# The token router before the expert stage: handovers between TensorE, VectorE and ScalarE put in another order

## The reference, cut to what matters

```
def hier_moe(h, wg, bg, we, be, w_gate, w_up, w_down):
    t = h.reshape(B * L, D)
    p_group = softmax(t @ wg + bg)                  # 4 groups
    p_top_g, g_idx = top_k(p_group, 1)
    e_logits = (einsum('td,gde->tge', t, we) + be)  # 8 experts of the chosen group
    e_logits = take_along_axis(e_logits, g_idx[:, :, None], axis=1)[:, 0]
    p_top_e, e_idx = top_k(softmax(e_logits), 2)
    w_sel = p_top_g * p_top_e / sum(p_top_e)
    combine = ...                                   # w_sel put at (token, group, expert)
    for gi in range(4):
        hid = silu(t @ w_gate[gi]) * (t @ w_up[gi]) * combine[:, gi]
        out = out + hid @ w_down[gi]
```

## Time and profile before

| what | value |
|---|---|
| median of 3 runs | 1753.59 us (1751.63 to 1757.33) |
| the profiled execution | 1757.33 us, its span 1755.5 us |
| granted TensorE clock, mean | 0.933 of full speed |
| PE busy | 1573.2 us (90%) |
| DVE busy | 487.9 us (28%) |
| ACT busy | 341.3 us (19%) |
| HBM | 226 GB/s over the span |

### The profile page before, as it was taken

The page is one execution under the profiler, slowest core; times in us unless marked ns, Lnnn a source line. Parts: engine busy times, 40 slices in busy tenths (PEclk is TensorE's granted clock), DMA queues, the critical chain, the costliest instruction groups (busy, mean ns, idle before and its releaser), DMA issues.

```text
span 1755.5 us, 21937 instructions
## 1 busy us (share of the span) xinstructions
PE 1573.2 (90%) x9261; PEld 1070.7 (61%) x9261; DVE 487.9 (28%) x1221; ACT 341.3 (19%) x706; POOL 4.1 (0%) x8
## 2 busy tenths in 40 slices
PE   6999979899979879988998999958889999889797
PEld 3655768778765433734365654447666676767465
DVE  2200163452134321223114000035252231010681
ACT  2301240222122112011200000032212222111371
POOL 0000000000000000000000000000000000000000
PEclk9999995799979899989999999968999999989999
DMA  9989520122158998999999999822222323323000
GB/s 380 409 350 370 213 102 1 48 99 97 49 228 340 367 421 343 405 391 409 417 399 413 403 406 421 344 102 84 96 96 96 144 96 135 153 82 121 1 1 25
DMA packets 54303, 397.57 MB, mean 226 GB/s; under 512 B 6359, under 2 KB 13688, under 8 KB 16440
## 3 DMA queue, kind: packets, MB, share of 16 engines
q1 hardware_dynamic: 40384, 341.85, 48.6%
q10 hardware_dynamic: 13240, 52.16, 7.5%
q0 software_dynamic: 576, 2.10, 0.3%
HBM read 389.80 MB, written 6.29 MB: 226 GB/s over the span
## 4 chain that ended last, share of the span: by engine, by line
PE 77%; DMA 8%; DVE 6%; ACT 4%; issue 2%; PEld 1%; ACTq 1%; SPq 0%; PEldq 0%; DVEq 0%
PE bank L680 15%; PE bank L1416 12%; PE bank L1431 8%; PE bank L2345 7%; DMA work<-in_moe_w_up 4%; PE bank L2362 4%; PE bank L1531 3%; PE bank L1536 3%; PE bank L525 3%; PE bank L2331 2%; DMA work<-in_moe_w_gate 2%; PE bank L711 2%; PE bank L1140 2%; PE bank L1128 2%; PE bank L869 2%
## 5 line engine op out<-in xcount | busy, mean ns | idle before, releaser
L680 PE MATMUL bank<-H,ring 128*128 128x256 f32 (+1 forms) x928 | 243.4, 422 | 6.1 <-ACT work L1057 4.0
L680 PEld LDWEIGHTS bank<-H,ring 128*128 128x128 f32 x928 | 176.9, 192 | 65.3 <-issue 41.4
L2345 PE MATMUL bank<-ring,work 128*32 128x512 f32 (+1 forms) x768 | 141.4, 639 | 17.2 <-DMA work<-in_moe_w_up 7.8
L1416 PE MATMUL bank<-H,work 128*128 128x256 f32 x512 | 114.1, 381 | 0.5 <-issue 0.5
L1416 PE MATMUL bank<-H,ring 128*128 128x256 f32 x512 | 113.0, 381 | 0.0
L1416 PEld LDWEIGHTS bank<-H,work 128*128 128x128 f32 x512 | 96.0, 190 | 19.0 <-issue 6.6
L1416 PEld LDWEIGHTS bank<-H,ring 128*128 128x128 f32 x512 | 98.1, 192 | 13.7
L2345 PEld LDWEIGHTS bank<-ring,work 128*32 128x32 f32 (+1 forms) x768 | 37.0, 123 | 108.7 <-issue 86.6
L1431 PE MATMUL bank<-work,H 128*128 128x512 f32 x192 | 85.2, 597 | 0.0
L1431 PE MATMUL bank<-ring,H 128*128 128x512 f32 x192 | 83.0, 592 | 0.0
L2345 PE MATMUL bank<-work 128*32 128x512 f32 (+1 forms) x256 | 68.9, 688 | 3.7 <-DMA work<-in_moe_w_up 3.7
(11 more groups left out here) (404 smaller groups left out, 2003.6 us busy)
## 6 DMA issues: line engine op xcount, KB each, us to landing
ring<-in_moe_w_gate SPq DMA_DIRECT2D x48, 1024.0 KB, 11.2
ring<-in_moe_w_up SPq DMA_DIRECT2D x48, 1024.0 KB, 9.1
ring<-in_moe_w_down SPq DMA_DIRECT2D x48, 1024.0 KB, 12.0
work<-in_ab_w_in ACTq DMA_DIRECT2D x28, 1024.0 KB, 10.3
ring<-in_ab_w_in SPq DMA_DIRECT2D x14, 2048.0 KB, 7.5
work<-in_ada_w SPq DMA_DIRECT2D x12, 2048.0 KB, 15.7
ring<-in_w_in SPq DMA_DIRECT2D x12, 2048.0 KB, 10.0
work<-in_w_mod SPq DMA_DIRECT2D x12, 2048.0 KB, 8.8
```

The costliest lines, as they stand in the source:

```text
L680: mm = nc.tensor.matmul(bank[i % NB][:, 0:n], weight(c, k, j * P, (j + 1) * P), rhs(k), start=(k == 0), stop=(k == kt - 1))
L1416: mm = nc.tensor.matmul(b[:, j * T:(j + 1) * T], w_k(m, n, k, at, at + P), H[:, k, m.s], start=(k == 0), stop=(k == DT - 1), skip_group_ch ...
L2345: mm = nc.tensor.matmul(bank[b][rows, :], gath[:, k, rows], half_slot[(load_at[n + half] + e) % NHALF][:, (k % 4) * 512:(k % 4 + 1) * 512] ...
```

## The change

On PE, the first tile of the second block's work (8 products) goes ahead of the counts and places, the second tile goes ahead of the key's transposition, the places come before the counts and have no release of their own (`place_mm` is given once), the three transpositions (key and `by_expert`) stand together, and the products by `ranked` (those for `place` and `comb_s`, and those for `ids`) stand together too. On ACT, the take of the gates and of the first pair of tiles comes before the exponential of `r3`. On DVE, the group's weight is computed behind the first exponential, `comb` and `by_expert` are computed behind `member_out` and ahead of the key, and `by_lane` is copied with the ranks, so that DVE and PE exchange two handovers fewer (`lane_mm` and `lane_out` end at 2).

```diff
@@ router_pe
             next(head)
+            next(head)
 
             pe.wait_ge(tables_in, 32)
             pe.wait_ge(member_out, 1)
+            nc.tensor.matmul(bank[0][:, 0:NX], tri, member[:, 0, :], start=True, stop=True)
+            nc.tensor.matmul(bank[0][:, NX:2 * NX], ones[:], member[:, 0, :], start=True, stop=False, skip_group_check=True)
+            nc.tensor.matmul(bank[0][:, NX:2 * NX], tri, member[:, 1, :], start=False, stop=True, skip_group_check=True)
             nc.tensor.matmul(bank[1][:, 0:NX], ones[:], member[:, 0, :], start=True, stop=False)
             nc.tensor.matmul(bank[1][:, 0:NX], ones[:], member[:, 1, :], start=False, stop=True).then_inc(place_mm, 1)
...
+            next(head)
             pe.wait_ge(hrow_out, 4)
             pe.wait_ge(lane_out, 1)
...
+            nc.tensor.transpose(bank[2][0:2 * NX, 0:P], key_row, ident[:])
             for t in range(TT):
-                mm = nc.tensor.transpose(bank[2][0:2 * NX, t * P:(t + 1) * P], by_expert[:, t, :], ident[:])
+                mm = nc.tensor.transpose(bank[3][0:2 * NX, t * P:(t + 1) * P], by_expert[:, t, :], ident[:])
             mm.then_inc(lane_mm, 1)
             next(head)
-            pe.wait_ge(lane_out, 4)
+            pe.wait_ge(lane_out, 2)
...
+            nc.tensor.matmul(bank[0][:, 4 * NX:5 * NX], bc(vec("lane")[0:NX, :], [NX, P]), ranked[0:NX, :], start=True, stop=True, skip_group_check=True)
+            nc.tensor.matmul(bank[0][:, 5 * NX:6 * NX], bc(key_col[0:NX, :], [NX, P]), ranked[0:NX, :],
+                             start=True, stop=True, skip_group_check=True).then_inc(lane_mm, 1)
             for _ in head:
                 pass
@@ router_act
             nc.scalar.activation(ex4, ex4, ACT.Exp).then_inc(rt_e, 1)
+            head = head_act(act)
+            next(head)
             act.wait_ge(rt_x, 2)
             nc.scalar.activation(r3, r3, ACT.Exp).then_inc(rt_e, 1)
-            head = head_act(act)
@@ router_dve
             V.tensor_tensor(ex4, g4, bc(r1, s4), ALU.subtract).then_inc(rt_x, 1)
+            dve.wait_ge(rt_e, 1)
+            L(V.tensor_reduce(r2[:, :, 0], ex4, AXX, ALU.add))
+            L(V.reciprocal(r2, r2))
             for g in range(NG):
...
             ins.then_inc(member_out, 1)
+            dve.wait_ge(rt_e, 2)
+            L(V.tensor_scalar(r1, r3, 1.0, None, ALU.add))
+            L(V.reciprocal(r1, r1))
+            L(V.tensor_tensor(r2, r2, r1, ALU.mult))
...
+            for g in range(NG):
+                L(V.tensor_tensor(comb[:, :, g * NE:(g + 1) * NE], oh1, bc(oh4[:, :, g:g + 1], s8), ALU.mult))
             dve.wait_ge(place_mm, 1)
+            L(V.tensor_tensor(by_expert[:, :, 0:NX], bank[0][:, 0:2 * NX].rearrange("p (t e) -> p t e", e=NX), member, ALU.mult))
+            L(V.tensor_copy(by_expert[:, :, NX:2 * NX], comb))
+
             L(V.scalar_tensor_tensor(out=key_row[:, 0:NX], in0=bank[1][:, 0:NX], scalar=float(NX), in1=slot_no[:, 0:NX], op0=ALU.mult, op1=ALU.subtract))
             V.tensor_copy(key_row[:, NX:2 * NX], key_row[:, 0:NX]).then_inc(lane_out, 1)
             dve.wait_ge(lane_mm, 1)
...
             L(V.tensor_reduce(rank[both, :], above[both, :], AXX, ALU.add))
+            L(V.tensor_copy(by_lane[both, :], bank[3][both, 0:T]))
             V.tensor_scalar(ranked[both, :], slot_no[both, 0:NX], rank[both, :], None, ALU.is_equal).then_inc(lane_out, 1)
             dve.wait_ge(lane_mm, 2)
...
```

More of the change, by code:

```diff
@@ L2036, in router_pe @@
             next(head)
+            next(head)
             pe.wait_ge(tables_in, 32)
             pe.wait_ge(member_out, 1)
+            nc.tensor.matmul(bank[0][:, 0:NX], tri, member[:, 0, :], start=True, stop=True)
+            nc.tensor.matmul(bank[0][:, NX:2 * NX], ones[:], member[:, 0, :], start=True, stop=False, skip_group_check=True)
+            nc.tensor.matmul(bank[0][:, NX:2 * NX], tri, member[:, 1, :], start=False, stop=True, skip_group_check=True)
             nc.tensor.matmul(bank[1][:, 0:NX], ones[:], member[:, 0, :], start=True, stop=False)
             nc.tensor.matmul(bank[1][:, 0:NX], ones[:], member[:, 1, :], start=False, stop=True).then_inc(place_mm, 1)
-            nc.tensor.matmul(bank[0][:, 0:NX], tri, member[:, 0, :], start=True, stop=True)
-            nc.tensor.matmul(bank[0][:, NX:2 * NX], ones[:], member[:, 0, :], start=True, stop=False, skip_group_check=True)
-            nc.tensor.matmul(bank[0][:, NX:2 * NX], tri, member[:, 1, :], start=False, stop=True, skip_group_check=True).then_inc(place_mm, 1)
+            next(head)
             pe.wait_ge(hrow_out, 4)
             pe.wait_ge(lane_out, 1)
[L2048 to L2055, removed]
+            nc.tensor.transpose(bank[2][0:2 * NX, 0:P], key_row, ident[:])
             for t in range(TT):
-                mm = nc.tensor.transpose(bank[2][0:2 * NX, t * P:(t + 1) * P], by_expert[:, t, :], ident[:])
+                mm = nc.tensor.transpose(bank[3][0:2 * NX, t * P:(t + 1) * P], by_expert[:, t, :], ident[:])
             mm.then_inc(lane_mm, 1)
             next(head)
-            pe.wait_ge(lane_out, 4)
+            pe.wait_ge(lane_out, 2)
             for t in range(TT):
@@ L2063, in router_pe @@
                     rows = slice(half * NX, (half + 1) * NX)
-                    mm = nc.tensor.matmul(bank[half][:, t * NX:(t + 1) * NX], by_lane[rows, t * P:(t + 1) * P], ranked[rows, :],
-                                          start=True, stop=True, skip_group_check=True)
-            mm.then_inc(lane_mm, 1)
+                    nc.tensor.matmul(bank[half][:, t * NX:(t + 1) * NX], by_lane[rows, t * P:(t + 1) * P], ranked[rows, :],
+                                     start=True, stop=True, skip_group_check=True)
+            nc.tensor.matmul(bank[0][:, 4 * NX:5 * NX], bc(vec("lane")[0:NX, :], [NX, P]), ranked[0:NX, :], start=True, stop=True, skip_group_check=True)
+            nc.tensor.matmul(bank[0][:, 5 * NX:6 * NX], bc(key_col[0:NX, :], [NX, P]), ranked[0:NX, :],
+                             start=True, stop=True, skip_group_check=True).then_inc(lane_mm, 1)
             for _ in head:
@@ L2126, in router_dve @@
             ins.then_inc(member_out, 1)
+            dve.wait_ge(rt_e, 2)
+            L(V.tensor_scalar(r1, r3, 1.0, None, ALU.add))
+            L(V.reciprocal(r1, r1))
+            L(V.tensor_tensor(r2, r2, r1, ALU.mult))
+            L(V.tensor_tensor(r3, r2, r3, ALU.mult))
+            L(V.tensor_tensor(oh1, oh1, bc(r2, s8), ALU.mult))
+            L(V.tensor_tensor(oh2, oh2, bc(r3, s8), ALU.mult))
+            L(V.tensor_tensor(oh1, oh1, oh2, ALU.add))
+            for g in range(NG):
+                L(V.tensor_tensor(comb[:, :, g * NE:(g + 1) * NE], oh1, bc(oh4[:, :, g:g + 1], s8), ALU.mult))
             dve.wait_ge(place_mm, 1)
+            L(V.tensor_tensor(by_expert[:, :, 0:NX], bank[0][:, 0:2 * NX].rearrange("p (t e) -> p t e", e=NX), member, ALU.mult))
+            L(V.tensor_copy(by_expert[:, :, NX:2 * NX], comb))
             L(V.scalar_tensor_tensor(out=key_row[:, 0:NX], in0=bank[1][:, 0:NX], scalar=float(NX), in1=slot_no[:, 0:NX], op0=ALU.mult, op1=ALU.subtract))
@@ L2134, in router_dve @@
             L(V.tensor_reduce(rank[both, :], above[both, :], AXX, ALU.add))
+            L(V.tensor_copy(by_lane[both, :], bank[3][both, 0:T]))
             V.tensor_scalar(ranked[both, :], slot_no[both, 0:NX], rank[both, :], None, ALU.is_equal).then_inc(lane_out, 1)
             dve.wait_ge(lane_mm, 2)
-            L(V.tensor_copy(ids, bank[3][:, 0:NX]))
-            L(V.tensor_scalar(last_col[:, 0:1], bank[3][:, NX:NX + 1], float(NX * CAP_WIDE + 1), None, ALU.is_ge))
-            L(V.tensor_scalar(last_col[:, 1:2], bank[3][:, NX + N_WIDE:NX + N_WIDE + 1], float(NX * CAP_SLIM + 1), None, ALU.is_ge))
+            L(V.tensor_copy(ids, bank[0][:, 4 * NX:5 * NX]))
+            L(V.tensor_scalar(last_col[:, 0:1], bank[0][:, 5 * NX:5 * NX + 1], float(NX * CAP_WIDE + 1), None, ALU.is_ge))
+            L(V.tensor_scalar(last_col[:, 1:2], bank[0][:, 5 * NX + N_WIDE:5 * NX + N_WIDE + 1], float(NX * CAP_SLIM + 1), None, ALU.is_ge))
             V.tensor_tensor(over, last_col[:, 0:1], last_col[:, 1:2], ALU.max).then_inc(ids_out, 1)
[L2141 to L2157, removed]
             L(V.tensor_scalar(place.rearrange("p t e -> p (t e)"), bank[0][:, 0:2 * NX], -1.0, None, ALU.add))
```

## The result

The changed kernel is slower: 1763.61 us against 1752.61 us (medians of 6 runs each), a ratio of 1.0063 with a 95% interval of 1.0035 to 1.0091. A second comparison, with more runs of the kernel before, gave 1.0055 (1.0033 to 1.0077). That is a loss of 9.6 to 11 us where +4.4 was forecast.

A forecast was written before the change was run, and what follows sets the result against it. The prediction took PE's own router work, ahead of an expert stage hanging on weight transfers, as the bound. Stall and starts +2.9, clock +1.5, weights 0 gave +4.4 us on 1753.6: 1758.0 us, range 1752.5 to 1763.

The forecast's parts named there:

- The first new wait: Router: DVE stands 4.1 us for the exponential of `ex4`; `member` still comes 0.8 us before PE wants it, costing nothing.
- The second new wait: Router: PE stands 4.1 us ahead of the key's transposition, behind `r3`'s late exponential; old 1.0 us stall goes; shift +2.9 us.
- The clock: Router: PE runs at half clock for a while behind the new stall, adding +1.5 us.
- The expert weights: First expert loads are issued 16 us later, but hidden before the expert steps need them: 0 us, bounds 0 and +2.
- rival (b): Expert stage: late weights collide and up weights queue behind gate weights; +7.5 us with a longer half-clock stretch, 1761 us; 25%.
- Rival (a): Router: PE's clock holds through the new stall, or falls only while PE stands; +2.9, 1756.5 us; 15%.
- Rival (c): Router: ACT runs `r3`'s exponential before the pair of tiles is done, so no new stall; -1.2, 1752.4 us; 5%.
- The test on the length of the expert stage: The forecast would be wrong if the stage from first gather to 1130 us changed length by more than 2 us.
- a microsecond won or lost in the router is passed on whole: Router: nothing in front of the first expert step can be made up for later, so router gains and losses reach the total.
- The table load: Router, ACT: the load takes 1.28 us with no drain behind it; an exposed drain would make the sum 0.6 us larger.

The follow-up runs named there:

- exp_first: The changed kernel with the exponential of `r3` put back ahead of ACT's takes of the gates and first pair of tiles; ratio 1.0030 to the kernel before.
- exp_first_late_f2: The changed kernel with the exponential of `r3` ahead of ACT's takes and ACT's two 1 MB loads behind the up weights; ratio 1.0000 to the kernel before.
- tail_only: The kernel before with one edit: ACT takes the router's last pair of tiles ahead of issuing its two 1 MB loads; ratio 1.0014.

## Why the prediction was wrong

**The first new wait is hidden**: right, with the cover used up to the last. DVE stood 4.07 us (4.1 forecast), and PE waited 0.15 us at L2041 where 0.8 us of cover were worked out. In this execution the gates and the first tile ended 0.7 us sooner from the router's start, at the same moment as `member`.

**The second new wait**: right in mechanism and size. PE stood 4.05 us (4.1 forecast), released by DVE behind ACT's exponential, and the 1.0 us for the ranks went.

**The clock**: right, a little small. It fell during the stall and came back at about 515.3 us. The third tile, from 510.92 to 516.63, took 5.7 us for 3.6: 2.1 us where 1.5 were taken. The gather moved by 4.9 us (41.10 less 36.17) for +4.4. The undoing of this part (exp_first) is worth 0.0025 to 0.0033 of the time, 4 to 6 us, though by the profiles it moves the gather by 6.7 us.

**The expert weights**: this is the step that failed. "So the 16 us cost nothing ... I take 0; the bounds are 0 and +2." The start of the weights moved by 38.6 - 22.1 = 16.5 us, as forecast, and PE waited for no gate weights in the first pass. But the wait for the up weights grew by 4.7 us. The step counted ten transfers of 1 MB and let the next ones begin with the up weights. There were twelve: ACT issues two more, 3.6 us ahead of the up weights, and in the kernel before they ran in the pause that I took for cover. The right count: the weights start 11.5 us later as seen from the gather, the pause is 6.5 us, and 5.0 are left to pay, an estimate; 4.7 were measured. The windows of before from 540 to 548 us had it, where the transfers resume at 545.5 us, 3 us ahead of the first issue of up weights at 548.46; I read SyncE's queue and not ACT's.

The term was named in rival (b), that the late weights collide, but priced at 1 to 2 us for want of those two loads, and set to begin at a shift of over 17 us, where 16.5 were enough. With 4.9 + 4.7 = 9.6 us the sum meets the 9.0 us by which the changed kernel is behind at the second gather, the 9.3 us at the end of the profile, and the 9.6 to 11 us of the times. The figure at the end is in part luck: the last two gathers of the expert stage lie 39.6 us apart in the profile of before and 36.8 in that of the changed kernel, and the part behind the stage is 2.5 us longer in the changed one. The range ended at 1763, with the measured 1763.6 just outside, and the forecast of a loss inside 0.3% was wrong.

**Rival (a)**, the clock holds, fell. **Rival (c)**, the exponential early: exp_first is that kernel, and its router is what (c) describes (34.4 us, no stall), yet it is 0.30% slower, since (c) too took the weights to be free. The test on the length of the expert stage is not clear. Up to the ninth of its ten gathers the stage is 4.5 us longer (529.3 against 524.8 us, and 528.7 in the second profile of the changed kernel), about as much as the wait; up to its last product it is only 1.8 us longer in the first profile (614.9 against 613.1) and 4.1 in the second. The first of these would have passed the test, so the wait for the up weights is what shows the failed step, not this length.

The premise that a microsecond won or lost in the router is passed on whole holds for the loss, and for a gain only up to the second gather: exp_first_late_f2 and tail_only are 2.9 us ahead of the kernel before there, and their times are not below it.

**The table load**: the Trainium skill's drain at a switch of tables (ScalarE: Activation LUTs, "What ACT_TABLE_LOAD costs") does not show here either. In the changed kernel ACT's copy ends at 494.49, the load runs from 494.50 for 1.28 us, and the exponential starts at 495.80, so that no 1380 ns of drain stand on either side of the load.

## What to carry to other kernels

A transfer that is moved is hidden only if the whole stream behind it still fits: count the bytes of every queue from its start to the next transfer that someone waits for, and look in the windows for the pause that pays. In an engine's list, a small operation that others wait for must not stand behind a take that waits for large work. And a gain at one place, or a distance in one profile, is not yet time: here the part ahead of the router scattered by 6 us from profile to profile, whatever the kernel, and the part behind it by 5 us for one and the same kernel.

## What the runs showed that I had not expected

A stop of PE of 2.58 us ahead of the gather left the clock at full in three of three profiles (32 instructions in 3.84 us), while stops of 3.04 us and more at the same place were followed by half clock in each of the nine other profiles (about 5.5 us).
